# A third seven-product chunk in each wide round of a two-block fp32 transformer kernel

## What is computed

```
def swiglu(h, w_in, w_out):
    gu = h @ w_in                      # 256x2048 by 2048x11264
    gate, up = gu[..., :D_FF], gu[..., D_FF:]
    return (jax.nn.silu(gate) * up) @ w_out     # 256x5632 by 5632x2048
```

## Time and profile before

| | |
|---|---|
| timed runs, median (lowest to highest) | 2668.81 us (2668.37 to 2668.97) |
| profiled execution | 2668.85 us |
| its span | 2667.1 us |
| PE busy | 2655.7 us (100%) |
| DVE busy | 1926.6 us (72%) |
| ACT busy | 1392.4 us (52%) |

### The profile page before, as it was taken

One profiled execution on the slowest core, in us unless ns is written; L12 is line 12 of the kernel. 1 busy time (PEld: TensorE's weight loads), 2 busy tenths in 40 slices (PEclk: granted clock), 3 DMA queues, 4 the chain that ended last, 5 costly groups with the idle time before them and its releaser, 6 DMA issues.

```text
span 2667.1 us, 32619 instructions
## 1 busy us (share of the span) xinstructions
PE 2655.7 (100%) x12038; PEld 2193.6 (82%) x12038; DVE 1926.6 (72%) x2464; ACT 1392.4 (52%) x1836; POOL 58.2 (2%) x64
## 2 busy tenths in 40 slices
PE   9999999999999999999999999999999999999999
PEld 7888888888888788888888888887888888888887
DVE  6888889886645466888888886758555576566566
ACT  6555555454544445555555454555554464675463
POOL 0000000000000000000000000030000000020000
PEclk9999999999999999999999999999999999999999
DMA  9767677677845466666576667755467576546754
GB/s 303 232 198 236 194 231 222 205 222 240 257 144 174 146 219 211 212 225 224 181 246 204 222 213 226 253 186 158 137 186 258 166 237 211 174 143 206 240 181 135
DMA packets 348575, 550.89 MB, mean 207 GB/s; under 512 B 40992, under 2 KB 120096, under 8 KB 347648
## 3 DMA queue, kind: packets, MB, share of 16 engines
q1 hardware_dynamic: 346624, 539.90, 63.4%
q0 software_dynamic: 1648, 8.86, 1.0%
q10 hardware_dynamic: 144, 0.04, 0.0%
HBM read 525.59 MB, written 23.07 MB: 206 GB/s over the span
## 4 chain that ended last, share of the span: by engine, by line
PE 98%; DMA 1%; SPq 0%; DVE 0%; ACT 0%; issue 0%; ACTq 0%; DVEq 0%
PE bank L1467 17%; PE bank L1469 17%; PE bank L1468 17%; PE bank L1536 14%; PE bank L1535 14%; PE bank L1534 14%; DMA raw<-in_ffn_w_in_dram 1%; PE bank L1426 1%; PE bank L1134 0%; PE bank L886 0%; PE bank L870 0%; PE bank L1114 0%; PE bank L568 0%; PE bank L840 0%; SPq L1315 0%
## 5 line engine op out<-in xcount | busy, mean ns | idle before, releaser
L1965 DVE TENSOR_TENSOR wlo<-raw,whi 128x1024 fp32r<-128x1024 f32 (+3 forms) x559 | 641.9, 1158 | 542.8 <-ACT whi L1616 537.8
L1616 ACT CAST whi<-raw 128x1024 fp32r<-128x1024 f32 (+3 forms) x559 | 548.9, 990 | 649.5 <-PE bank L1469 623.8
L1756 ACT CAST whi<-raw 128x1024 fp32r<-128x1024 f32 (+1 forms) x416 | 409.2, 998 | 413.3 <-PE bank L1536 405.8
L2125 DVE TENSOR_TENSOR wlo<-raw,whi 128x1024 fp32r<-128x1024 f32 (+1 forms) x416 | 463.3, 1150 | 67.3 <-ACT whi L1756 64.9
L1467 PE MATMUL bank<-whi,p_hi 128*128 128x512 f32 x1184 | 465.6, 393 | 3.1 <-DVE wlo L1965 3.1
L1469 PE MATMUL bank<-whi,p_lo 128*128 128x512 f32 x1184 | 461.1, 389 | 0.0
L1468 PE MATMUL bank<-wlo,p_hi 128*128 128x512 f32 x1184 | 460.9, 389 | 0.0
L1467 PE MATMUL bank<-whi,q_hi 128*128 128x512 f32 x864 | 340.6, 394 | 0.5 <-DVE wlo L1965 0.5
L1469 PE MATMUL bank<-whi,q_lo 128*128 128x512 f32 x864 | 336.6, 390 | 0.0
L1468 PE MATMUL bank<-wlo,q_hi 128*128 128x512 f32 x864 | 336.3, 389 | 0.0
L1467 PEld LDWEIGHTS bank<-whi,p_hi 128*128 128x128 f32 x1184 | 222.4, 188 | 52.7 <-issue 5.7
(11 more groups left out here) (381 smaller groups left out, 2984.6 us busy)
## 6 DMA issues: line engine op xcount, KB each, us to landing
raw<-in_ffn_w_in_dram SPq DMA_DIRECT2D x704, 256.0 KB, 3.8
raw<-in_ffn_w_out_dram SPq DMA_DIRECT2D x320, 256.0 KB, 4.0
raw<-in_w_in_a_dram SPq DMA_DIRECT2D x192, 256.0 KB, 3.1
raw<-in_w_in_mix_dram SPq DMA_DIRECT2D x128, 256.0 KB, 3.2
raw<-in_w_ple_gate_dram SPq DMA_DIRECT2D x128, 256.0 KB, 3.7
raw<-in_w_in_b_dram SPq DMA_DIRECT2D x128, 256.0 KB, 3.1
raw<-in_w_out_mix_dram SPq DMA_DIRECT2D x64, 256.0 KB, 3.3
raw<-in_w_o_a_dram SPq DMA_DIRECT2D x64, 256.0 KB, 3.7
```

The lines of the kernel that those rows point to most:

```text
L1616: act.copy(whi[:, c % SPLIT, 0:n, 0:w], raw[:, c, 0:n, 0:w]).then_inc(hi_done, 1)
L1756: act.copy(whi[:, i % SPLIT, 0:n, :], raw[:, i % CH, 0:n, :]).then_inc(hi_done, 1)
L1965: dve.tensor_tensor(wlo[:, c % SPLIT, 0:n, 0:w], raw[:, c, 0:n, 0:w], whi[:, c % SPLIT, 0:n, 0:w].bitcast(F32), ALU.subtract).then_inc(lo_ ...
L2125: dve.tensor_tensor(wlo[:, i % SPLIT, 0:n, :], raw[:, i % CH, 0:n, :], whi[:, i % SPLIT, 0:n, :].bitcast(F32), ALU.subtract).then_inc(lo_d ...
```

## The change

Chunks 1, 3 and 5 of each wide round go by seven products instead of 2 and 5; buffers for sums hold three sets; an operand set more is made for each stage (`in0`: three in a plain round; `out`: one in `in` w2, one in `in` w3, one in `out` w0, at c = 4 and 5). The sums of chunk 1 are made between the two halves of `evacuate_wide`, the sums of chunks 3 and 5 after the two `wlo` of their chunk, and SP's load over those units waits for them as well. The ACT casts of the sums of chunks 3 and 5 stand behind the cast of the next unit. The hidden columns are split in two instructions of 512 columns instead of four of 256, at c = 6 instead of 5. `combine_products` stands ahead of the `wlo` of unit 14. The scratch for software DMAs is set to 8192 bytes.

```diff
-SEVEN = (2, 5)
+SEVEN = (1, 3, 5)
...
                         sp.wait_ge(lo_done, unit_at(s, wide, i) + 1)
+                        if unit_at(s, wide, i) - CH in summed_units:
+                            sp.wait_ge(t24_sum, summed_units[unit_at(s, wide, i) - CH] + 1)
...
             def wide_round(s, wide):                      # ACT
                 n = wides.index((s.name, wide))
+                sums_13_hi(s, wide, SEVEN[0])
+                sums_24_hi(s, wide, SEVEN[0])
                 for c in range(2, CH):
                     wide_hi(s, wide, 2 * c)
+                    if c - 1 in SEVEN[1:]:
+                        sums_13_hi(s, wide, c - 1)
+                        sums_24_hi(s, wide, c - 1)
...
                 else:                                     # DVE, begin_wide
-                    evacuate_wide(before[0], before[2])
+                    evacuate_wide(before[0], before[2], (0,))
+                    weight_sums(s, wide, SEVEN[0])
+                    evacuate_wide(before[0], before[2], (1,))
...
             def wide_round(s, wide):                      # DVE
                 before = ahead_of(s, 2 * wide)
+                weight_sums_lo(s, wide, SEVEN[0])
                 for c in range(2, CH):
+                    if c == CH - 1:
+                        combine_products(s, wide)
+                    wide_lo(s, wide, 2 * c)
+                    wide_lo(s, wide, 2 * c + 1)
+                    if c == 2 and before[2] is not None:
+                        finish_wide(before[0], before[2])
                     if c in SEVEN:
                         weight_sums(s, wide, c)
-                    wide_lo(s, wide, 2 * c)
-                    if c == CH - 1:
-                        combine_products(s, wide)
-                    wide_lo(s, wide, 2 * c + 1)
-                    if c in SEVEN:
                         weight_sums_lo(s, wide, c)
...
                     if c == 4:
                         if s.kind == "ffn_out" and wide == 0:
-                            operand_sums_lo(s, 1)
+                            operand_sums(s, 2)
-                        if s.kind == "ffn_in" and wide == 3:
-                            operand_sums_lo(after(s, 2 * wide)[0], 0)
+                        if s.kind == "ffn_in" and wide in (2, 3) and s.name[-1] != "2":
+                            operand_sums(by_name[s.name.replace("in", "out")], wide - 2)
...
-                    if c == 5:
+                    if c == 6:
                         for s_, k_ in halves_behind(s, wide):
                             hidden_lo(s_, k_, k_ % 2)
```

More of the change, by code:

```diff
@@ L485, in unit_at @@
             return (s.r0 + 2 * wide) * CH + i
+        summed_units = {unit_at(s, wide, 2 * c + n): seven_number(s, wide, i) for s, _, wide in flat if wide is not None
+                        for i, c in enumerate(SEVEN) for n in range(2)}
         def unit_tiles(i):
@@ L1658, in hidden_hi @@
                 act.wait_ge(hid_moved[u], moved_by(s, k, u))
[L1659 to L1662, removed]
+                act.copy(pair_hi[s.hid_pair][:, k * 2:k * 2 + 2, :].rearrange("p j (t q n) -> p (j t) q n", t=TT, q=4),
+                         hidf[:, u, :, :, :, :].rearrange("p q j t n -> p (j t) q n")).then_inc(hid_hi, 1)
             def block_hi(s, k):
@@ L1803, in wide_round @@
                     wide_hi(s, wide, 2 * c + 1)
-                    if c in SEVEN:
-                        weight_sums_hi(s, wide, SEVEN.index(c))
-                    if c == 3:
+                    if c == 4:
                         if s.kind == "ffn_out" and wide == 0:
-                            operand_sums_hi(s, 1)
-                        if s.kind == "ffn_in" and wide == 3:
-                            operand_sums_hi(after(s, 2 * wide)[0], 0)
-                    if c == 5:
+                            operand_sums_hi(s, 2)
+                        if s.kind == "ffn_in" and wide in (2, 3) and s.name[-1] != "2":
+                            operand_sums_hi(by_name[s.name.replace("in", "out")], wide - 2)
+                    if c == 6:
                         for s_, k_ in halves_behind(s, wide):
@@ L1887, in second_half @@
                             x_squares(0)
-                        if s.name[-3:] == "in0" and k == 1 and c >= 6:
-                            operand_sums_hi(s, c - 6)
+                        if s.name[-3:] == "in0" and k == 1 and c >= 5:
+                            operand_sums_hi(s, c - 5)
                         if peeled:
@@ L2002, in hidden_lo @@
                 dve.wait_ge(hid_hi, s.hid0 + k + 1)
[L2003 to L2007, removed]
+                hi_, lo_ = (pair[s.hid_pair][:, k * 2:k * 2 + 2, :].rearrange("p j (t q n) -> p (j t) q n", t=TT, q=4)
+                            for pair in (pair_hi, pair_lo))
+                dve.tensor_tensor(lo_, hidf[:, u, :, :, :, :].rearrange("p q j t n -> p (j t) q n"), hi_.bitcast(F32),
+                                  ALU.subtract).then_inc(hid_done, 1)
             def block_lo(s, k):
@@ L2128, in weight_sums @@
             def weight_sums(s, wide, c):
-                i = SEVEN.index(c)
-                q = seven_number(s, wide, i)
+                q = seven_number(s, wide, SEVEN.index(c))
+                a_ = 2 * c % CH
+                for n in range(2):
+                    dve.wait_ge(landed[a_ + n], (s.r0 + 2 * wide + 2 * c // CH) * 32 + 32)
                 if q:
@@ L2179, in combine_products, with evacuate_wide @@
                 link(dve.tensor_tensor(y_, w_, p7, ALU.add))
-            def evacuate_wide(s, wide):
-                for n in range(2):
+            def evacuate_wide(s, wide, blocks):
+                for n in blocks:
                     dve.wait_ge(chunk_used, unit_at(s, wide, 14 + n) + 1 + USED0)
@@ L2338, in round_ @@
                             operand_lo(s, b, u)
-                        if s.name[-3:] == "in0" and k == 1 and c < 6:
+                        if s.name[-3:] == "in0" and k == 1 and c < 7:
                             operand_sums(s, c - 4)
                         if s.name[-3:] == "in0" and k == 1 and c == CH - 1:
-                            for i in range(2):
+                            for i in range(3):
                                 operand_sums_lo(s, i)
```

49 lines of the change are left out of this document (23 added, 26 removed).

## The result

The changed kernel took **2712.03 us** (median of four runs, 2710.36 to 2712.58) against 2668.62 for the kernel before on the same chip: a ratio of 1.0161, interval 1.0149 to 1.0174. That is slower, as forecast, but by 43.4 us in place of 23, and 8 us above the top of the range. The profiled execution took 2712.15 us with a span of 2710.4.

What follows compares the result with a forecast made beforehand. PE bounds the kernel as a whole, but DVE would bound the class 1 rounds: +28.6 - 9.5 + 2.4 + 1.4 + 0.5 = +23.4 us on 2668.85, forecast 2692 us; own range 2685 to 2701, widened to 2681 to 2704.

Steps and rivals of the forecast that it cites:

- The hidden columns at c = 6: In `out0` w0 and `out1` w0 DVE waits 0.3 to 0.4 us for PE: +1.4 us over four rounds.
- class 1: Twelve wide rounds with hidden columns and an operand set: DVE needs 44.55 us, +2.38 each, +28.6 us in all.
- ACT term: Class 1, chunks 3 and 5: DVE waits 0.1 us for ACT's cast of the sums, 24 times, +2.4 us.
- The 1.64 us: DVE's wait behind the operand set in class 1, for ACT's cast of the next unit; claimed not fillable.
- rival B: The operand wait of 1.64 us in class 1 is filled: 2672.6 us, no measurable change; chance 0.07.
- The two waits of the earlier trace: DVE's waits in `in0` w3 for PE's units 15 and 14, 1.43 and 0.36 us; both can be filled.
- rival C: At chunks 3 and 5 DVE waits for ACT's casts of the sums: 17 us more, 2709 us; chance 0.11.
- Classes 2 and 3: Wide rounds with hidden columns alone (4), or neither or first of SwiGLU (10): gain 0.68 us each, -9.5 us.
- the first wide round of each SwiGLU: Counted in class 3, as a round where DVE has room: gains 0.68 us.
- the SP trip: Hidden columns leave and come back, wanted about one chunk later: costed at 0, up to 1 us a round if late.
- the third operand set: In the plain round, 2.46 us of DVE ahead of `in0` w1's first `wlo`, mostly covered: +0.5 us, between 0 and 2.46.
- Rival A: PE stays the bound everywhere, so only the 17.7 us of fewer matmuls count: 2651 us; chance 0.07.

Runs made afterwards that it cites:

- Experiment 1: Changed kernel with the low part of the third operand set ahead of chunk 5's sums on DVE, in `out` w0 only: 2694.92 us, ratio 1.0099.
- experiment 3: Changed kernel with ACT casting the operand set after unit 10 instead of before it: 2692.19 us, ratio 1.0087.
- experiment 2: Changed kernel with the hidden columns back at c = 5 on ACT and DVE: 2716.62 us, ratio 1.018.
- experiment 4: Changed kernel with three chunks in 14 wide rounds, two in 12 (hidden columns there at c = 5), one operand set fewer per `out` stage: 2670.82 us, ratio 1.0007.
- experiment 6: Changed kernel, three chunks in all 26 rounds, with the edits of experiment 1 and experiment 3 together: 2676.3 us, ratio 1.0029.
- Experiment 5: Kernel of experiment 4 with chunk 5 of two-chunk rounds in the old order on DVE and ACT, and the angles later: 2664.12 us, ratio 0.9983.

## Why the forecast was wrong in its size

**The step that failed is "The hidden columns at c = 6".** It priced what PE waits for in `out0` w0 and `out1` w0, and came to 0.35 us a round for the hidden columns alone. It missed the other thing that had moved behind the sums in these same rounds: `operand_sums_lo`, from c = 4 to behind the sums of chunk 5. The prediction counted the operand set as DVE time, but put PE's wait for it at nothing, without a reason, although by its own class 1 DVE is late in just these rounds. What the runs show in its place is a wait of 5.33 to 5.38 us at the start of chunk 5, with a granted clock of 0.5 behind it. Experiment 1 shows its worth: 16.0 us in four rounds, of the 20 that the sum was short.

The hidden columns themselves were priced too low, but within the bounds: where experiment 1 lets them show, a round is 0.75 us longer than class 1. (The prediction's own figures, 9.9 less 9.65, give 0.25 and not 0.35.) In the changed kernel PE shows no wait for them, since it comes late from chunk 5.

**Class 1 was right**: 44.50 us measured, 44.55 worked out from the rows before the ACT term. The 1.64 us stayed, as the earlier trace rows had it, so rival B fell; experiment 3 took it away and left 42.96. The two waits of the earlier trace rows were filled as said: the evacuations at 187.38 and 191.17 have none ahead of them, and the sums of chunk 1 stand between.

**The ACT term of +2.4 us was mis-sized, downward.** The second low part of the sums starts 1.19 us after the first (218.18 to 219.37) in place of the 1.14 of the earlier trace rows, some 0.05 in place of 0.1, and in the rounds of `in` stages nothing of the term shows over 44.55. In class 1 rival C did not come: DVE was the late one there, as argued against it. In `in1` w1 (class 2) DVE does wait 0.58 us for the cast of the sums, ahead of 347.05, and the round stays at 41.50.

**Classes 2 and 3 were right**, but for the first wide round of each SwiGLU: 41.50, worked out 41.48. DVE was busy 40.23 of the 41.50 in `in1` w1 and had the room. The two instructions of 512 columns took 1.21 us from start to start (614.18 to 615.39), estimated 1.20. That the SP trip costs nothing held at c = 6, where ACT shows no wait for it; experiment 2 shows that one chunk earlier it would have cost 0.7 to 1.8 us in each class 2 round.

**The first wide round of each SwiGLU was mis-sized**, and the third operand set has little part in it. For the set the prediction had +0.5. The second plain round's evacuation comes 15.55 us after the first's in place of 15.34 (42.16 to 57.71, before 41.16 to 56.50), so the set costs 0.2 there, and in the second SwiGLU DVE still has a wait left over. But the prediction counted the round behind it as one with room, -0.68. In this round the sums of chunk 1 come behind the evacuation, where DVE has no wait for them to fill, and ahead of the `wlo` for which PE waits (0.72 and 1.00 us), and in the first SwiGLU the angles stand ahead of the low sums (1.25 us). From the first plain evacuation to the first wide one all kernels with this code take 56.20 to 56.24 us (the changed kernel and experiments 1 to 4 and 6), against 53.92 before: +2.3 where -0.68 was due from PE. Experiment 5, which moved the angles, takes 54.84. That the sums of chunk 1 cause the other wait is read from the rows; no run moved them. The second SwiGLU lost 1.3 us at the same place, where I had none. Equal kernels differ by up to 1.7 us ahead of all this: the first plain evacuation comes at 40.48 in experiment 3 and at 42.16 in the changed kernel after waits of PE for `wlo` of 1.11 us (ended at 31.43) and 2.38 us (at 33.13).

**Rival A** is refuted, as the prediction thought likely. The Trainium skill, "Perfetto Trace Analysis", section "Identifying the Most-Contended Engine", has one improve the engine with the highest occupancy first, and for TensorE judge the headroom by its share of peak FLOPs or by the busy share of its weight loads. By the busy shares that is PE here (matmuls 100%, weight loads 82%, against 72% for DVE). It got 17.7 us less work, and the kernel became 43.4 us slower.

**Two more slips of arithmetic** change nothing in this. The likely bounds that the prediction lists add to at least +12 and to -6, that is to 2686 and 2704, and not to the 2685 to 2701 that it states. And a third chunk has five new DVE instructions (three sums, two low parts), not six; the 0.2 us named for them holds for five.

## What to carry to other kernels

When work is moved behind other work on an engine that will be late, list every semaphore that the moved instructions release, and for each find the instruction that waits and whether it opens a whole block of work or a part of it: 0.68 us of DVE cost 16 here because PE's wait stood at the head of a chunk. Take an engine's room round by round, by its instructions plus the waits that can't be filled, and apply a change only in the rounds that have it: with the orders mended, the third chunk makes the kernel 0.29% slower when it stands everywhere and 0.17% faster when it stands only where there was room. An in-order engine that serves two consumers should do first what is ready, not what still waits for a transfer (experiments 2, 4 and 5).

## What I had not expected of the hardware

After the wait of 5.33 us the matmuls of `out0` w0 started 0.43 us apart (221.86 to 224.42, six of them) and only then 0.2267 again; the window from 221.30 to 226.00 shows a granted clock of 0.64, a mean over both levels. In the second SwiGLU, after a wait of 5.38 us, a stretch lies wholly at half clock (1.2 of 2.4 GHz); the window of that piece of `out0` w0:

```profile
1249.90:1254.00 4.10, 4.10 (x10) 3.23 (x11) 3.37 (x4) 1.06 (x2) 0.00 (x0) 0.50 0.77 262
```

So the long wait was paid twice, with 1.69 us on top in the first case. With the waits of experiment 1 in the same round, at most 1.39 us long, the granted clock was 1.00.

The length of the wait alone does not decide it. In experiment 3 PE waits 3.78 to 3.80 us in each of the four `out` w0 rounds; after three of these waits the clock fell (rounds of 48.39, 47.05 and 46.99 us), after the fourth it did not (45.58). In the changed kernel a wait of 2.38 us in a plain round, ended at 33.13, was also followed by seven starts 0.43 us apart; after one of 1.82 us, ended at 32.13 in the kernel before, the granted clock was 1.00.
